# HGRN2 in a hybrid encoder layer: where filling matmuls stand among the seven levels of the score computation

## The reference

```python
def hgrn2(f_pre, i_in, q_in, g_in, lb, norm_w):
    log_f = jnp.logaddexp(jnp.log(lb), jnp.log1p(-lb) + jax.nn.log_sigmoid(z))
    key = (1.0 - lb) * jax.nn.sigmoid(-z)
    def chunk_step(state, inp):                       # chunks of 64 tokens
        qc, kc, vc, lfc = inp
        b = jnp.cumsum(lfc, axis=2)
        rel = jnp.where(causal[:, :, None], b[:, :, :, None, :] - b[:, :, None, :, :], -jnp.inf)
        scores = jnp.einsum('bhqd,bhkd,bhqkd->bhqk', qc, kc, jnp.exp(rel))
        o_intra = jnp.einsum('bhqk,bhkv->bhqv', scores, vc)
        o_inter = jnp.einsum('bhqd,bhdv->bhqv', qc * jnp.exp(b), state)
        ...
    g = jax.nn.silu(g_in.astype(jnp.float32)).reshape(Bn, Sn, HG_HEADS, HG_DIM)
    return (rms_norm(o, norm_w) * g).reshape(Bn, Sn, HG_WIDTH)
...
merged = g_a * (o_a @ w_branch_a[l]) + g_b * (o_b @ w_branch_b[l]) + g_c * (o_c @ w_branch_c[l])
```

## The kernel before

| place | sc 1 | sc 2 | sc 3 | sc 4 | sc 5 | sc 6 | sc 7 | past | left | tok 0 | tok 1 | tok 2 | tok 3 | ss |
|---|---|---|---|---|---|---|---|---|---|---|---|---|---|---|
| parts | 28a | 28b | 29a | 29b | 30a | 30b | 31a | 31b, 32 | 33 | 34 | 35 | 36 | 37 | 38, 39 |

## Time and profile before

### The profile page before, as it was taken

The page is one execution under the profiler, slowest core; times in us unless marked ns, Lnnn a source line. Parts: engine busy times, 40 slices in busy tenths (PEclk is TensorE's granted clock), DMA queues, the critical chain, the costliest instruction groups (busy, mean ns, idle before and its releaser), DMA issues.

```text
span 1082.2 us, 19329 instructions
## 1 busy us (share of the span) xinstructions
PE 1044.0 (96%) x8229; PEld 835.2 (77%) x8229; DVE 612.5 (57%) x858; ACT 449.0 (41%) x575; POOL 30.8 (3%) x50
## 2 busy tenths in 40 slices
PE   7999999999999999999989999999999999999997
PEld 5788676777776787787767778888888888878885
DVE  3489887356444479668655297762445432342346
ACT  5522742233324476756455553471222122323233
POOL 0100001000000000020000100000000000000000
PEclk9999999999999999999999999999999999999999
DMA  9978533111026321296312584304443423232202
GB/s 338 324 245 261 174 107 131 69 55 61 24 93 235 133 86 60 65 307 222 108 39 79 161 323 167 117 20 156 129 144 117 156 78 117 78 102 93 102 15 78
DMA packets 106781, 145.31 MB, mean 134 GB/s; under 512 B 3252, under 2 KB 86440, under 8 KB 106696
## 3 DMA queue, kind: packets, MB, share of 16 engines
q1 hardware_dynamic: 93544, 109.25, 30.6%
q0 software_dynamic: 5664, 21.19, 5.8%
q10 hardware_dynamic: 7488, 13.63, 3.3%
HBM read 128.33 MB, written 15.73 MB: 133 GB/s over the span
## 4 chain that ended last, share of the span: by engine, by line
PE 79%; DVE 10%; ACT 5%; DMA 2%; issue 2%; SPq 1%; ACTq 0%; POOL 0%; DVEq 0%
PE bank L2200 78%; DVE wlo L1462 2%; DVE Z L1462 1%; DMA raw<-in_w_in 1%; DVE q_lev L1462 1%; DMA qk<-early_out 1%; DVE BK L1462 1%; DVE near L1944 1%; SPq L810 1%; ACT whi L938 1%; ACT gate_row L953 1%; DVE mg L1462 1%; DVE ada_acc L1465 0%; DVE qk L1462 0%; PE bank L2783 0%
## 5 line engine op out<-in xcount | busy, mean ns | idle before, releaser
L2200 PE MATMUL bank<-hhi,whi 128*128 128x512 f32 (+1 forms) x800 | 319.7, 400 | 4.2 <-ACT gate_row L953 2.6
L2200 PE MATMUL bank<-hhi,wlo 128*128 128x512 f32 (+1 forms) x800 | 308.8, 386 | 0.0
L2200 PE MATMUL bank<-hlo,whi 128*128 128x512 f32 (+1 forms) x800 | 308.6, 386 | 0.0
L1462 DVE TENSOR_TENSOR wlo<-raw,whi 128x2048 fp32r<-128x2048 f32 (+1 forms) x80 | 166.3, 2079 | 233.7 <-ACT whi L938 227.1
L938 ACT ACTIVATE whi<-raw 128x2048 fp32r<-128x2048 f32 (+1 forms) x76 | 135.4, 1782 | 227.3 <-PE bank L2200 178.2
L2200 PEld LDWEIGHTS bank<-hhi,whi 128*128 128x128 f32 x800 | 150.2, 188 | 46.3 <-issue 10.9
L2200 PEld LDWEIGHTS bank<-hhi,wlo 128*128 128x128 f32 x800 | 150.3, 188 | 31.0
L2200 PEld LDWEIGHTS bank<-hlo,whi 128*128 128x128 f32 x800 | 150.4, 188 | 28.3 <-issue 0.7
L2200 PE MATMUL bank<-whi,d_hi 128*128 128x512 f32 x160 | 62.3, 390 | 1.2 <-DVE hid L1462 1.2
L2200 PE MATMUL bank<-whi,d_lo 128*128 128x512 f32 x160 | 62.3, 389 | 0.0
L2200 PE MATMUL bank<-wlo,d_hi 128*128 128x512 f32 x160 | 62.2, 389 | 0.0
(11 more groups left out here) (370 smaller groups left out, 1491.3 us busy)
## 6 DMA issues: line engine op xcount, KB each, us to landing
raw<-in_w_in SPq DMA_DIRECT2D x33, 1024.0 KB, 5.4
raw<-in_f_in SPq DMA_DIRECT2D x22, 1024.0 KB, 5.0
raw<-in_ada_w SPq DMA_DIRECT2D x16, 1024.0 KB, 5.0
early_out<-gate_row ACTq DMA_DIRECT2D x52, 256.0 KB, 2.4
raw<-in_f_out SPq DMA_DIRECT2D x11, 1024.0 KB, 4.8
cond<-in_ada_w SPq DMA_DIRECT2D x8, 1024.0 KB, 11.0
sg<-early_out POOLq DMA_DIRECT2D x4, 1536.0 KB, 11.7
raw<-in_w_out SPq DMA_DIRECT2D x4, 1024.0 KB, 5.0
```

The costliest lines, as they stand in the source:

```text
L1462: return v.tensor_tensor(out_, a, b, op)
L2200: return t.matmul(out_, lhsT, rhs, start=start, stop=stop, skip_group_check=True)
```

## The change

Levels 2 and 6 get three parts in place of two, and the place `hg ss` gets two in place of four. The number of parts in the stretch stays 40, so nothing moves outside it.

```diff
-    [(("hg z", 0), 4), (("hg z", 1), 4)] + [(("hg sc", lev), 2) for lev in range(1, LEVELS + 1)]
-    + [("hg past", 4), ("hg left", 2)] + [(("hg tok", c), 2) for c in range(TB)] + [("hg ss", 4), ("hg end", 0)],
+    [(("hg z", 0), 4), (("hg z", 1), 4)] + [(("hg sc", lev), 3 if lev in (2, 6) else 2) for lev in range(1, LEVELS + 1)]
+    + [("hg past", 4), ("hg left", 2)] + [(("hg tok", c), 2) for c in range(TB)] + [("hg ss", 2), ("hg end", 0)],
```

## The result

The changed kernel takes 1092.56 us (median of 6 runs, 1091.03 to 1095.01), the kernel before 1086.72 in the runs beside it (6 runs, 1083.93 to 1088.05). The ratio is 1.0059, with a 95% interval of 1.0046 to 1.0071: slower by 5.8 us. The profiled execution took 1092.43 with a span of 1090.4, so it is 8.2 us longer than that of before (1082.2). The two figures differ because the profiled execution of before was one of its fast ones (mean clock 0.999, 1084.3 us) and that of the changed kernel an ordinary one (0.994, with six runs between 0.993 and 0.997).

What follows compares the result with a forecast made beforehand. PE, busy 96% of the span, bounds the kernel, DVE paces the levels. Levels -2.7, bank 7 and panel +2.5, square +0.45, bank 4 +2.2, third scores +2.3: net +4.8; 1085.5 with +4.7 gives 1090.2, range 1085.5 to 1093.5.

Steps and rivals of the forecast that it cites:

- Levels: Levels 2 and 6: two added parts go into PE's pauses, hiding about 2.7 us, with the last scores still at 446.55.
- Bank 7: At hg past, unit 33 waits 2.43 us for ACT's copy of unit 31; the next panel adds another 0.1.
- Square: At hg ss, PE waits 0.4 to 0.5 us for ACT's squares, behind the first da v panel's split; +0.45 in the sum.
- bank 4: Inside da v, token block 2 waits 2.2 us for ACT's third logarithm, held by the queries' product.
- DVE's order: From tok 3, the first da v panel's low part precedes the queries' rotary products on DVE; keys' products begin +4.8 us.
- rest of the wait for the third scores: Ahead of the third scores, PE waits +2.3 us more at the end of the DVE and ACT chain.
- The keys' load: Behind the last output, the load shifts by 2.6 us and lands at 491.4, ahead of the keys' rotary products.
- rival (d): Clock falls to 1.2 GHz behind a new pause, 2.7 us more per 12 matmuls: 1093 to 1096; chance 0.03.
- The base: Whole kernel before: put at 1085.5 us, halfway between the profiled execution and the median of three timed runs, 2.35 above it.
- (c): Levels 2 or 6 don't absorb the parts; PE's scores hold DVE's pick, up to 2.7 us more: 1093; chance 0.03.
- (a) to (c): Three rivals; the middle one, behind the levels: less DVE and ACT lateness, between 0 and +3.2, 1085.5 to 1088.7; chance 0.20.
- (a): Fill hidden at levels 2 and 6, nothing late behind them: 2.7 us faster, 1082.8 by the base; chance 0.06.

Runs made afterwards that it cites:

- parts from past and early copies: Kernel before with levels 2 and 6 at three parts, the two parts taken from hg past, and ACT copying unit 31 out ahead of its copies into ST: 0.9970.
- DVE's order back: Changed kernel, but DVE makes the low part of the first da v panel behind the queries' rotary products again; ACT's order stays changed: 1.0007.
- early copies: Changed kernel, but ACT copies unit 31 out of bank 7 and splits the next panel ahead of the copies into ST, unit 32's copy between: 1.0034.
- parts from past, ACT untouched: Kernel before with levels 2 and 6 at three parts, the two parts taken from hg past, ACT's order unchanged: 1.0007.
- both orders back: Changed kernel with the first da v panel split behind the square on ACT and behind the queries' rotary products on DVE: 1.0018.
- kernel before, pause alone: Kernel before with ACT repeating two and a half copies into ST ahead of unit 31's copy, for a PE pause of 2.4 us: 1.0033.
- kernel before, double pause: Kernel before with five extra half copies into ST on ACT ahead of unit 31's copy, for a PE pause of 5 us: 1.0067.

## Why the prediction was right, and where its size was off

**Levels.** Right: the last scores came no later than the 0.3 us that were there before the levels, and 2.7 us of fill found room. The run with the parts from past and early copies shows it as time won.

**Bank 7.** Right in place and size: 2.24 us of pause where 2.43 were forecast, ended by the copy that stands behind the copies into `ST`. The 0.1 us for the next panel didn't show.

**Square and bank 4.** 0.25 in place of 0.45, 1.79 in place of 2.2. Both right in kind; the first a bit small since the fill ahead of it took slightly longer than I had.

**DVE's order.** Right, and the largest item as said. The "rest of the wait for the third scores", 2.3, is there as pauses of 0.48 and 1.98 less the old 0.27. The forecast had `q_rot` at 484.3 and `k_rot` at 493.55. With the 0.3 of offset and 1.6 of slow clock ahead of them these become 486.2 and 495.45; the trace has 486.15 and 495.45. The third scores: 515.3 and the same 1.9 give 517.2, measured 517.20.

**The keys' load.** It was put at 491.4. It was issued at 482.46 and landed 7.7 us later, at 490.2, where the load of before took 10.7 us. It decided nothing, but the later estimate for the run with DVE's order back leaned on it and was 3.6 us too high. A time from issue to landing that was read once, in a stretch with much other traffic, is not a constant.

**The clock.** This is the term that was mis-sized. The prediction kept it as rival (d) with a chance of 0.03, while the sum had none of it. In the profiled execution it came twice, 1.6 and 1.45 us, which is the whole difference between 4.8 and 8.2 (with the 0.3 of offset). Over all runs the medians moved by 5.8 (5.0 to 7.7 by the interval), so about 1 us beyond the sum. That would fit a fall in some executions only; how often it comes in the timed runs isn't shown. Rival (d) itself priced a fall too high: it had 2.7 us for every 12 matmuls, and a fall took 1.4 to 1.9 in all. The reason given for leaving it out, that a pause of 1.50 us had left the clock at 1.00, says nothing of pauses of 1.8 to 2.4. The trace of before does have a longer one, in the mixer ahead of this stretch, and it would have misled further, for one execution can't rule the fall out: ```profile
183.15 1.15 PE L2200 MATMUL bank<-cst,V 64*64 64x64 f32 x32 [2.28 <-DVE M L1735]
```

Behind it the clock stayed at 1.00. The same place in the changed kernel's profile, where nothing differs, had the clock at 0.60 and 0.54 in the two stretches from 182 to 186:

```profile
182.54 1.97 PE L2200 MATMUL bank<-cst,V 64*64 64x64 f32 x32 [2.29 <-DVE M L1735]
```

**The base.** The forecast of 1090.2 lies 2.4 us below the measured 1092.56. About half of that is no matter of the change: the base was put at 1085.5, and the kernel before measured 1086.72. The range reached far enough since its upper end was made for (c) and (d).

The rivals (a) to (c) didn't happen. (a) had as its decisive point the copy at 453.19 [rows 5]; moving it alone gave 1.0034, and only with the orders back as well does the changed table come out faster (0.9986).

## What to carry to other kernels

Work that fills pauses is hidden only while the things that it takes (here a bank behind a copy, and a split panel) are free at the new time; look for the margin of each, a copy that was 0.34 us early here, before moving it. A table that several engines walk moves instructions on all of them: one VectorE instruction that went ahead of a longer chain cost more, here about one and a half times as much, than the pause on TensorE that was easy to see. Take the filler from a place ahead of the next critical handoff rather than from one behind it: with the early copies, taking it from past brought the whole chain forward (0.9970) with no further edit, while taking it from ss lost time (1.0034) until both orders were put back, and then won less (0.9986).

## What the runs showed of the hardware

The granted clock fell to half behind pauses of 1.14 us to 4.97, and did so in some executions only, at the same place and with the same pause:

| profiled execution | pause, us | clock behind it |
|---|---|---|
| changed kernel, bank 7 | 2.24 | fell, 0.88 over 448 to 462 |
| parts from past, ACT untouched | 2.24 | fell, 0.89 over 448 to 464 |
| DVE's order back | 2.25 | 1.00 |
| both orders back | 2.26 | 1.00 |
| kernel before, pause alone | 2.39 | 1.00 |
| kernel before, double pause | 4.97 | fell, 0.79 over 448 to 464 |
| changed kernel, bank 4 | 1.79 | 1.00 |
| early copies, bank 4 | 1.77 | fell, 0.89 over 484 to 500 |
| changed kernel, third scores | 1.98 | fell, 0.81 over 512 to 520 |
| six executions, at 182 to 184 us | 2.28 to 2.29 | fell, 0.91 over 180 to 200 |
| the other four, same place | 2.28 | 1.00 |
| parts from past (both versions), at 30 us | 1.14 | fell, 0.91 over 20 to 40 |
| both orders back, same place | 1.14 | 1.00 |
| the other seven, same place | 1.04 to 1.13 | 1.00 |

The last five rows are places that no version changes, so the kernel before is exposed to the same falls; the shortest pause with one behind it is the 1.14 us of the version with parts from past and early copies:

```profile
29.64 0.69 PE L2216 MATMUL bank<-hhi,whi 128*128 128x512 f32 x1 [1.14 <-DVE wlo L1478]
30.13 0.63 PE L2216 MATMUL bank<-hlo,whi 128*128 128x512 f32 x1
```

In the stretch of the change each fall took 1.4 to 1.9 us of PE's time (1.5 to 1.6 behind bank 7 and 1.45 at the third scores in the changed kernel, 1.6 in two other versions, 1.9 behind the double pause), and behind the pauses of 2.24 us it set in only after the matmuls had run at full speed again for a microsecond or more. The Trainium skill (TensorE: Matmul & The Clock Gate, Why this matters for your kernels) states that idle stretches between bursts bring the half clock back. The trace agrees in kind (0.88, 0.89, 0.81 and 0.79 behind a pause), but not in every execution. What decides it for one and the same pause the runs don't show. Where a pause of this length can't be avoided, its price is its length and perhaps more: the runs with the pause alone give 3.7 us by the medians against 2.3 by the stretch, an estimated 1.4 us more, but the interval (2.2 to 5.1 us) doesn't exclude nothing.
